# Two of sixteen experts' rows spread over the tokens by TensorE, and row pairs combined by diagonal weights, in a two-layer decoder kernel

## What is computed

```python
def hierarchical_moe(h, wc, bc, wf, bf, w_gate_up, w_down):
    ...
    e_logit, e_idx = lax.top_k(fine_sel, TOP_K_INNER)
    e_w = jax.nn.softmax(e_logit, axis=-1) * g_prob
    ...
    gu = jnp.einsum('nd,edf->nef', xt, w_gate_up)
    gate, up = jnp.split(gu, 2, axis=-1)
    act = jax.nn.silu(gate) * up * gates.astype(h.dtype)[..., None]
    return jnp.einsum('nef,efd->nd', act, w_down).reshape(b, t, d)

def reference(x, norm_mix_w, norm_ffn_w, ...):
    for layer in range(DEPTH):
        ...
        x = x + mix
        h = rms_norm(x, norm_ffn_w[layer])
        x = x + hierarchical_moe(h, router_c_w[layer], ...)
    return rms_norm(x, final_norm_w)
```

## Time and profile before

| | |
|---|---|
| three runs | 1181.15 us median (1179.62 to 1185.16) |
| the profiled execution | 1181.09 us, span 1179.3 us |
| PE, DVE, ACT, POOL busy | 94%, 59%, 52%, 34% of the span |
| mean granted PE clock | 0.973 of full |
| DMA moved | 194.76 MB, 165 GB/s mean |

### The profile page before, as it was taken

The page is one execution under the profiler, slowest core; times in us unless marked ns, Lnnn a source line. Parts: engine busy times, 40 slices in busy tenths (PEclk is TensorE's granted clock), DMA queues, the critical chain, the costliest instruction groups (busy, mean ns, idle before and its releaser), DMA issues.

```text
span 1179.3 us, 19724 instructions
## 1 busy us (share of the span) xinstructions
PE 1111.8 (94%) x7062; PEld 912.1 (77%) x7063; DVE 701.5 (59%) x1016; ACT 608.6 (52%) x903; POOL 405.1 (34%) x344
## 2 busy tenths in 40 slices
PE   8999999999998899998999999999999997999980
PEld 5778887778787688886788888888888886888870
DVE  5435444367736999996646341543442138999975
ACT  5556234242434699995633342233342234899871
POOL 4343121110133244442155325442244442344442
PEclk8999999999999899999999999999999997999995
DMA  9333311112225699996443213331222364999955
GB/s 262 79 86 56 72 38 55 37 44 66 72 68 210 244 353 375 379 364 238 174 128 98 81 56 106 97 106 56 81 73 91 104 190 161 354 388 374 358 208 223
DMA packets 89859, 194.76 MB, mean 165 GB/s; under 512 B 20348, under 2 KB 21432, under 8 KB 89016
## 3 DMA queue, kind: packets, MB, share of 16 engines
q1 hardware_dynamic: 67560, 159.34, 40.6%
q10 hardware_dynamic: 12432, 17.60, 4.4%
q0 software_dynamic: 9792, 16.80, 3.8%
HBM read 189.50 MB, written 23.07 MB: 180 GB/s over the span
## 4 chain that ended last, share of the span: by engine, by line
PE 80%; DVE 8%; DMA 5%; ACT 3%; issue 2%; ACTq 1%; SPq 0%; POOL 0%; POOLq 0%; DVEq 0%
PE ps L674 23%; PE ps L676 22%; PE ps L675 22%; PE ps L2570 2%; PE ps L2362 2%; DMA raw<-in_moe_w_down_dram 1%; DMA arena<-y 1%; DVE x L1467 1%; PE ps L2245 1%; ACTq L1421 1%; PE ps L2498 1%; DMA arena<-hs,slot_rows 1%; PE ps L2199 1%; ACT wh L1007 1%; DMA y<-arena,cur_rows 1%
## 5 line engine op out<-in xcount | busy, mean ns | idle before, releaser
L841 POOL TENSOR_TENSOR wl<-raw,wh 128x1024 fp32r<-128x1024 f32 x94 | 228.6, 2440 | 380.5 <-ACT wh L1007 380.2
L674 PE MATMUL ps<-wh,hT_hi 128*128 128x512 f32 x864 | 346.7, 401 | 3.5 <-DVE hT_lo L1986 2.4
L676 PE MATMUL ps<-wh,hT_lo 128*128 128x512 f32 x864 | 337.9, 391 | 0.0
L675 PE MATMUL ps<-wl,hT_hi 128*128 128x512 f32 x864 | 337.2, 390 | 0.0
L1007 ACT ACTIVATE wh<-raw 128x1024 fp32r<-128x1024 f32 x116 | 122.4, 1068 | 212.6 <-PE ps L676 191.0
L674 PEld LDWEIGHTS ps<-wh,hT_hi 128*128 128x128 f32 x864 | 162.8, 188 | 39.1 <-issue 3.5
L676 PEld LDWEIGHTS ps<-wh,hT_lo 128*128 128x128 f32 x864 | 162.3, 188 | 34.6
L675 PEld LDWEIGHTS ps<-wl,hT_hi 128*128 128x128 f32 x864 | 162.8, 188 | 30.9
L674 PE MATMUL ps<-hT_hi,wh 128*128 128x512 f32 (+1 forms) x296 | 116.9, 395 | 2.1 <-DVE arena_rounded L1818 1.0
L1961 DVE TENSOR_TENSOR wl<-arena,wh 128x1024 fp32r<-128x1024 f32 x96 | 113.8, 1222 | 4.7 <-ACT wh L1294 3.1
L1961 DVE TENSOR_TENSOR wl<-raw,wh 128x1024 fp32r<-128x1024 f32 x92 | 109.5, 1223 | 8.2 <-ACT wh L1294 5.4
(11 more groups left out here) (331 smaller groups left out, 1576.8 us busy)
## 6 DMA issues: line engine op xcount, KB each, us to landing
raw<-in_moe_w_gate_up_dram SPq DMA_DIRECT2D x64, 512.0 KB, 11.5
arena<-in_moe_w_gate_up_dram SPq DMA_DIRECT2D x64, 512.0 KB, 10.5
raw<-in_odd_w_in_dram SPq DMA_DIRECT2D x48, 512.0 KB, 3.7
raw<-in_even_w_in_dram SPq DMA_DIRECT2D x32, 512.0 KB, 4.8
arena<-in_moe_w_down_dram SPq DMA_DIRECT2D x32, 512.0 KB, 11.7
raw<-in_moe_w_down_dram SPq DMA_DIRECT2D x32, 512.0 KB, 14.1
raw<-in_odd_w_out_dram SPq DMA_DIRECT2D x16, 512.0 KB, 3.6
arena<-y ACTq DMA_DIRECT2D x6, 1024.0 KB, 9.9
```

Source lines behind the costliest of these rows:

```text
L674: nc.tensor.matmul(dst, lh, rh, start=first, stop=False)
L675: nc.tensor.matmul(dst, lh, rl, start=False, stop=False)
L676: return nc.tensor.matmul(dst, ll, rh, start=False, stop=last)
L841: pool.tensor_tensor(columns_of(i, wl[:, i % NSPL, :, :]), raw_columns(i), columns_of(i, wh[:, i % NSPL, :, :]).bitcast(F32), ALU.subtract ...
```

## The change

Experts 14 and 15 (`LAST` = 14) are no longer stored by slots. ACT (high part) and DVE (`late_low`, L1540 of the changed kernel) scale their down result with each slot's weight `w_slot`, and PE (`late_rows`) spreads them over a token tile by products with one-hot matrices `slot_token` (eight fp32r matmuls 128x512 for a tile). DVE adds that from PSUM to x (`add_late`, L1547). The rows of experts 0 to 13 are still stored and loaded; `w_early` is w12 with zeros for experts 14 and 15, whose rows in `y2_dram` are filled with zeros by two indirect stores (`no_rows`). The slots' weights come by way of DRAM: ACT stores w12 after expert 1, POOL gathers it behind its first two experts (`late_experts`). SP issues the loads of the early rows after expert 13's store (`load_early_rows`). In layer 0 both keep_busy are gone and the low halves of pieces 0 and 1 of block 10 go from DVE to POOL. In layer 1 tiles 2 and 3 are not combined by DVE: PE multiplies the loaded rows by diagonal matrices of the weights, in fp32 (four matmuls 128x512 for a tile), ahead of the eight others in the same PSUM banks. The gathers of the two unused overflow columns and the waits that hung on them are gone.

```diff
-    return i in DVE_LO or any(m + 2 <= i < m + 6 * NE for m in MOE_PIECE) or first_piece(10) <= i < first_piece(10) + 4
+    return i in DVE_LO or any(m + 2 <= i < m + 6 * NE for m in MOE_PIECE) or first_piece(10) + 2 <= i < first_piece(10) + 4
...
+        YP = [reg(at, 2048).rearrange("p (j d) -> p j d", j=2) for at in (12288, 14336, 2048, 4096)]
+        no_rows = reg(15360, 1024)
+        late_hi, late_lo = v3(rounded(9216, 2048), 2), v3(rounded(7168, 2048), 2)
...
+            def load_early_rows(l):
+                for q in range(2):
+                    sp.wait_ge(s_(f"y_stored{q}"), 112 * (l + 1))
+                sp.wait_ge(s_("late_ready"), 64 * (l + 1))
+                sp.wait_ge(s_("slot_token_made"), 2 * (l + 1))
+                src = y2_dram[l].rearrange("(T p j) d -> T p j d", p=P, j=2)
+                sp.dma_start(YP[0][:, 0, :], src[0][:, 0, :]).then_inc(s_("yp_loaded0"), 16)
+                sp.dma_start(YP[0][:, 1, :], src[0][:, 1, :]).then_inc(s_("yp_second0"), 16)
+                for T in range(1, NT):
+                    sp.dma_start(YP[T], src[T]).then_inc(s_(f"yp_loaded{T}"), 16)
...
+                def late_experts():
+                    pool.wait_ge(s_("w_stored"), 16 * (l + 1))
+                    for e in range(2):
+                        rows = idx[:, 1, LAST + e:LAST + e + 1].bitcast(U32)
+                        pool.indirect_dma_start(out=w_slot[:, e:e + 1], out_offset=None, in_=w_dram[l],
+                                                in_offset=bass.IndirectOffsetOnAxis(ap=rows, axis=0),
+                                                bounds_check=last_pair_row, oob_is_err=False).then_inc(s_("late_ready"), 16)
+                    for e in range(2):
+                        rows = idx[:, 1, LAST + e:LAST + e + 1].bitcast(U32)
+                        pool.indirect_dma_start(out=y2_dram[l], out_offset=bass.IndirectOffsetOnAxis(ap=rows, axis=0),
+                                                in_=no_rows, in_offset=None,
+                                                bounds_check=last_pair_row, oob_is_err=False).then_inc(s_("late_ready"), 16)
...
+                    if l == 1 and last and par == 1:
+                        for T in (2, 3):
+                            for j in range(2):
+                                n = 2 * T + j
+                                act.activation(pair_diagonal(T, j), ident[:, :], ACT.Copy, scale=w_early[:, n:n + 1]).then_inc(s_("pair_diagonals"), 1)
+                    if last and par == 1:
+                        hi(m + 6 * NE)
+                        hi(m + 6 * NE + 1)
                     act.wait_ge(s_("ysb_free"), E + 1)
+                    if last:
+                        act.wait_ge(s_("late_ready"), 64 * (l + 1))
                     for hf in range(2):
+                        c = slice(512 * hf, 512 * hf + 512)
                         act.wait_ge(used, it * 12 + (6 * NE * l + 6 * par + 4 + n0 + hf + 1))
-                        act.activation(ysb[:, par, 512 * hf:512 * hf + 512], ps[:, 2 + hf, :], ACT.Copy).then_inc(s_("y_read"), 1)
-                        if hf == 0 and not last:
+                        if last:
+                            act.activation(late_hi[:, par, c], ps[:, 2 + hf, :], ACT.Copy, scale=w_slot[:, par:par + 1]).then_inc(s_("y_read"), 1)
+                            continue
...
+                    if n == 1:
+                        act.wait_ge(s_("slot_token_made"), 2 * (l + 1))
+                        with nc.allow_non_contiguous_dma(reason="two weights of a token"):
+                            act.dma_start(w_dram[l].rearrange("(T p j) o -> p T (j o)", p=P, j=2), v3(w12, 4)).then_inc(s_("w_stored"), 16)
...
+            def late_low(l, e, hf):
+                c = slice(512 * hf, 512 * hf + 512)
+                dve.wait_ge(s_("late_ready"), 64 * (l + 1))
+                dve.wait_ge(s_("y_read"), 32 * l + 31 + 2 * e + hf)
+                stt(late_lo[:, e, c], ps[:, 2 + hf, :], w_slot[:, e:e + 1], late_hi[:, e, c].bitcast(F32), ALU.mult, ALU.subtract)\
+                    .then_inc(s_("late_low_made"), 1)
+            def add_late(l, T):
+                dve.wait_ge(s_("late_rows"), 4 * l + T + 1)
+                b = late_banks(l, T)
+                D(tt(v3(X[:, T, :], 2), v3(X[:, T, :], 2), ps[:, b:b + 2, :], ALU.add), s_(f"moe_added{l}"))
             def norm(n):
+                if n in (2, 4):
+                    l = n // 2 - 1
+                    combine(l, 0, 0)
+                    combine(l, 0, 1)
+                    late_low(l, 1, 0)
+                    late_low(l, 1, 1)
+                    combine(l, 1, 0)
+                    add_late(l, 0)
+                    combine(l, 1, 1)
+                    add_late(l, 1)
...
+                    lo_tiles(("hT", n, 0), 0)
                     for i in range(4):
                         lo(first_piece(10) + i)
-                    combine(0, 0, 0)
-                    combine(0, 0, 1)
-                    combine(0, 1, 0)
-                    combine(0, 1, 1)
-                    dve.wait_ge(s_("wb_loaded"), 32)
-                    for T in range(NT):
+                    for T in range(1, NT):
+                        if T + 1 < NT:
+                            combine(0, T + 1, 0)
+                            combine(0, T + 1, 1)
+                            add_late(0, T + 1)
                         lo_tiles(("hT", n, T), T)
-                        if T + 2 < NT:
-                            combine(0, T + 2, 0)
-                            combine(0, T + 2, 1)
...
+                    for T in (2, 3):
+                        add_late(1, T)
+                        last(T - 2)
...
+                D(dve.memset(w_slot, 0.0))
+                D(ts(slotB, slotA, 1, None, ALU.logical_shift_right))
+                D(ts(w_early, slotB, LAST // 2, None, ALU.not_equal))
+                D(tt(w_early, w_early, w12, ALU.mult))
+                D(tt(token_at, idx[:, 0, LAST:NE].unsqueeze(2).broadcast_to([P, 2, NT]),
+                     offs16[:, 0:NT].unsqueeze(1).broadcast_to([P, 2, NT]), ALU.subtract))
+            def slot_tokens():
+                for e in range(2):
+                    D(tt(v3(slot_token[e], NT), iotaB.unsqueeze(1).broadcast_to([P, NT, P]),
+                         token_at[:, e, :].unsqueeze(2).broadcast_to([P, NT, P]), ALU.is_equal), s_("slot_token_made"))
...
+                    if n == 0:
+                        slot_tokens()
...
+            def late_rows(l, T):
+                if T == 0:
+                    pe.wait_ge(s_("slot_token_made"), 2 * (l + 1))
+                elif T > 1 and l == 0:
+                    pe.wait_ge(s_(f"moe_added{l}"), T)
+                b = late_banks(l, T)
+                by_pe = l == 1 and T > 1
+                if by_pe:
+                    pe.wait_ge(s_("pair_diagonals"), 2 * (T - 1))
+                    pe.wait_ge(s_(f"yp_loaded{T}"), 16 * (l + 1))
+                    for j in range(2):
+                        for hf in range(2):
+                            mm(ps[:, b + hf, :], pair_diagonal(T, j), YP[T][:, j, 512 * hf:512 * hf + 512], start=j == 0, stop=False)
+                for e in range(2):
+                    pe.wait_ge(s_("late_low_made"), 4 * l + 2 * e + 2)
+                    for hf in range(2):
+                        c = slice(512 * hf, 512 * hf + 512)
+                        mm(ps[:, b + hf, :], slot_token[e][:, cols(T)], late_hi[:, e, c], start=e == 0 and not by_pe, stop=False)
+                        ins = mm(ps[:, b + hf, :], slot_token[e][:, cols(T)], late_lo[:, e, c], start=False, stop=e == 1)
+                ins.then_inc(s_("late_rows"), 1)
             def norm(n):
                 if n == 2:
-                    keep_busy(22)
+                    late_rows(0, 0)
+                    late_rows(0, 1)
                 for T in range(NT):
+                    if n == 2 and T == 1:
+                        late_rows(0, 2)
...
+                        if last and par == 1:
+                            pe.wait_ge(s_("late_low_made"), 4 * l + hf + 1)
```

130 lines of the change are left out of this document (76 added, 54 removed).

## The result

The changed kernel takes 1195.11 us (median of four runs, 1192.22 to 1195.85), the kernel before 1180.38 in the same comparison; the ratio is 1.0112, with a 95% interval of 1.0079 to 1.0144. So it is slower by 1.1%, and outside the predicted range. The profiled execution took 1195.85 us with a span of 1194.0, against 1179.3 before.

What follows compares the result with a forecast made beforehand. PE, busy 94% of the span, was taken as the bound, with DVE, ACT and DMA nearly full in the MoE. The sum was 1181.1 + 1.4 + 1.5 + 1.7 - 3.7 = 1182.0 us, range 1174 to 1187.5.

Steps and rivals of the forecast that it cites:

- The chain of the tails: From the last expert on: order of DVE, PE and POOL work, +1.5 us in layer 0 and -3.7 in layer 1.
- The clock's cost: Tail of layer 0: after 5.8 us idle PE's clock is down, twelve of 16 matmuls take 0.46 us each.
- the hold that the prediction took over from a row of 128x160: Tail of layer 0: POOL's low pieces hold DVE's first addition until 548.8 us; without hold it starts at 546.8.
- The stall by DVE at the start: Start of each MoE: DVE's five small operations and two comparisons delay PE by 1.4 us (0 to 2.3).
- the two signs: Prediction wrong if POOL's transfers make PE wait for a gather, or if the clock does not fall.
- Start, ACT and POOL: Start of each MoE: w12 store, POOL's transfers and zero rows cost 0 in layer 0, 0.3 us in layer 1.
- the slack of a gather: Start of each MoE: a later expert's gather comes 6 to 8.5 us late on POOL, within 9 us slack; cost 0.
- PE never has to wait for it twice for the same delay: Start of each MoE: DVE, with 0.38 us free in 10, catches up slowly, but its delay stalls PE only once.
- D: Slower rival: w12 store holds ACT 2.2 us, gather over 9 us late, 3 us a layer, 1188 us; chance 0.16.
- The condition that was to decide it: Start of each MoE: the slower rival decides when w_stored lands later than 7 us after its issue.

Runs made afterwards that it cites:

- w_store_long_runs: Changed kernel with w12 stored in 128 runs of 32 bytes in place of 512 of 8, so gathered weights are wrong; 1188.17 us, ratio 1.0083.
- no_late_transfers: Changed kernel without the store of w12, the gathers from it and the mixtures' zero rows (row buffers zeroed early); 1183.51 us, ratio 1.0026.
- keep_busy_9: Changed kernel with nine useless fp32 matmuls put back in layer 0's tail ahead of late_rows; 1191.39 us, ratio 1.0090.
- before_2mb: Kernel before with a 2 MB DRAM-to-DRAM copy issued by ACT after expert 1 of each mixture; 1190.58 us, ratio 1.0087.
- before_dve_ops: Kernel before with the change's five small operations and two comparisons added on DVE, results unread; 1186.34 us, ratio 1.0039.
- layer1 kernels: Layer 0 as in the kernel before, layer 1 with the change without zero rows; variants, among them 1185.38, 1181.50 and 1181.28 us.
- before_w_store: Kernel before with only ACT's store of w12 after expert 1 added, in 512 runs of 8 bytes, read by nobody; 1184.73 us, ratio 1.0038.
- layer1_best: Kernel before with the change in layer 1 only, no zero rows, tile 2 combined by DVE, DVE's seven operations moved late, w12 in 32-byte runs; 1181.28 us, ratio 0.9993.
- before_tile3_by_pe: Kernel before with tile 3 of layer 1's tail combined by two diagonals on PE behind 28 useless matmuls; 1181.46 us, ratio 0.9995.

## Why the prediction was wrong

The chain of the tails came out near in its sizes: in layer 0 PE was idle for 5.75 us (5.8 in the text) and +1.9 stands for +1.5, in layer 1 the fp32 products took 3.6 to 3.67 us for 3.5 and -3.9 stands for -3.7.

In layer 0 that is in part luck. The rows were to be there at +0.5 us, counted from the end of PE's last product, and DVE's first addition at +2.5, held until then by POOL's low piece. They landed at +2.7, later than POOL's end, so the idle time came out right by another wait. The clock's cost was to be twelve slow matmuls at once; seven were slow there and six behind tile 2. And the same tail took between 43.9 and 45.8 us in five kernels, so +1.9 could have been 0. In layer 1 the early rows were issued 5.4 us ahead of the last product and not some 11, which PE's longer work hid.

The changed kernel's own trace doesn't show whether POOL holds the addition, but three experiments do, in which the rows landed while POOL was at its last low piece. w_store_long_runs, POOL and DVE:

```profile
547.44 4.72 POOL L875 TENSOR_TENSOR wl<-raw,wh 128x1024 fp32r<-128x1024 f32 x2 [7.69 <-ACT wh L1060]
...
551.27 3.29 DVE L1533 SCALAR_TENSOR_TENSOR x<-arena,small,x 128x1024 f32<-128x1024 f32 x2 [3.75 <-DMA arena<-y]
```

The two additions took 3.29 us in place of 2.64. The first of them took 1.97 us here, 2.10 in no_late_transfers and 1.61 in keep_busy_9, in place of 1.28, and in all three it ended 1.1 us behind the end of POOL's piece. So the hold that the prediction took over from a row of 128x160 is there at 128x1024 too. The Trainium skill ("SBUF — State Buffer", "Who interferes with whom") says that a VectorE instruction with two SBUF inputs contends with a GpSimd instruction that reads SBUF. These three traces agree with it.

The stall by DVE at the start was right too, 1.5 for 1.4 at expert 2.

Neither of the two signs came that the prediction named for its being wrong, a wait of PE for a gather and a clock that stays up. The step that failed is the one under "Start, ACT and POOL": the zero rows and the store of w12 were costed at 0 for layer 0 and at 0.3 for layer 1, "in a stretch whose DMA share is 1.00". The text priced the store by ACT's time to issue it, and POOL's four transfers by the slack of a gather (that held: behind the first transposes of a mixture PE waited for no gather). It did not price the time of the transfer engines, nor what else stands behind POOL's wait for the store: the freeing of `ysb`, which cost 0.9 and 1.4 us. The earlier trace rows had shown the transfer engines full, and the earlier trace rows had shown ACT waiting for weights in the second mixture; the bytes alone (0.5 MB of zero rows a layer) were 1.4 us, against a slack that before_2mb puts at 1 us. The cost of the store could not have been read from its bytes: 4 KB. It shows in runs, 3.2 to 3.6 us a layer between 8-byte and 32-byte ones, POOL's part included.

Another sentence, "PE never has to wait for it twice for the same delay", is in doubt. before_dve_ops lost 3.0 and 2.5 for 1.4, half of it at the end, and 6.0 in its time; but MoE 1 of no_late_transfers bears the sentence out, with 1.0 lost in all. It stays open.

Added up, 3.0 (DVE), 3.6 (8-byte runs) and 2.4 (zero rows) make 9.0 for the first mixture, where 8.7 was measured, and 2.5, 3.2 and 2.3 make 8.0 for the second, where it was 8.3. The agreement is closer than the parts are known: each is from one profile, and the loss by POOL is in both of the last two. The layer1 kernels show that this sum is no law.

Of the rivals, D had the right sign and named the store of w12, but by ACT's issue (0.38 us, not 2.2) and by the late gather, 3 us a layer; both were wrong. It got 0.16. The condition that was to decide it, a landing more than 7 us after the issue, came true, with 9.0 and 8.3 us. POOL's lateness did reach PE, but through `ysb` and not through a gather, and for less than D said.

## What to carry to other kernels

Where a window shows two engines and the transfers full at once, price each added edit in all of them: in engine time, in transfer time and in the release of the buffers that the next load waits for. Where an engine has to wait for a transfer in its order, look at everything that stands behind that wait, not only at the next transfer. Transfer time lost there is paid at the end of the stretch, tens of microseconds behind its place, and on another engine than the one that it runs on; take the slack by one dummy transfer of known size. In a tail, split the additions so that DVE and PE end together (27.4 to 24.2 us here), and keep PE working through the wait ahead of its part (27.6 to 25.1 in the profiles, though the time did not show it). Before a stage of one profile is taken for an effect, look how far it differs between kernels that leave it alone.

## What the hardware did that was not expected

A store of 4 KB from 128 partitions in 512 runs of 8 bytes took 9.0 us to land, and in the six microseconds behind its issue the transfer engines moved 172 GB/s. Alone in the kernel before (before_w_store) it took 6.6 us, with 169 GB/s where the kernel before moved 325. In 128 runs of 32 bytes it took 4.5, with 300 GB/s. The queue of the small store itself has a share of 1.5% of the engines' time in 420 to 440, so it is the other queues' packets that take longer: from 423 to 432 the queue of the weights had 351 packets in 74.1% of the engines' time, 0.30 us each, and in the kernel before 949 packets in 80.1%, 0.12 us each. The Trainium skill ("DMA: Bandwidth & Descriptors", "Why small descriptors are slow (HBM only)") explains slow small descriptors by a fixed cost for each packet and 32 bytes of metadata for each operation. By that figure the store's metadata would be 16 KB, an estimate, 0.04 us at 375 GB/s. The traces here show a cost to others that this does not give.

PE's clock fell to 0.50 behind an idle time of 5.75 us in the changed kernel and of 3.76 in layer1_best, and did not behind one of 1.85 in the changed kernel's tail of layer 1. In layer 0, however, it stood at 0.50 from 579 to 581 us after an idle time of 1.79 us only, with PE busy since 561.71 but for waits of up to 0.8 us. It fell behind 1.79 us at the same place of keep_busy_9 too, behind 2.00 in the same tail of before_w_store and behind 1.88 in before_tile3_by_pe's, and stayed up behind 2.09 us in the kernel before's. So the length of the one idle time does not decide it in these traces; what does is open.
